# The dense first layers with one 512-column product for both parts of the values

## What is computed

```python
def swiglu(x, w1, w3, w2):
    return (jax.nn.silu(x @ w1) * (x @ w3)) @ w2

x = x + gate1 * diff_attention(h, ...)
h = rms_norm(x, norm2_g[0]) * (1.0 + scale2) + shift2
x = x + gate2 * swiglu(h, ffn_w1[0], ffn_w3[0], ffn_w2[0])
...
x = x + gate1 * gla_mixer(h, ...)
x = x + gate2 * moe_swiglu(h, ...)
```

## Time and profile before

| | |
|---|---|
| median of 3 runs | 1329.33 us (1327.12 to 1330.67) |
| the profiled execution, its own time | 1329.2 us |
| its span, first to last instruction | 1327.2 us |
| busy in the span: PE, DVE, ACT | 1277.0, 914.9, 733.9 us |
| mean granted clock of PE | 0.989 of full speed |
| first layers' dense part, about | 176 to 362 us of the span |

### The profile page before, as it was taken

The page is one execution under the profiler, slowest core; times in us unless marked ns, Lnnn a source line. Parts: engine busy times, 40 slices in busy tenths (PEclk is TensorE's granted clock), DMA queues, the critical chain, the costliest instruction groups (busy, mean ns, idle before and its releaser), DMA issues.

```text
span 1327.2 us, 20642 instructions
## 1 busy us (share of the span) xinstructions
PE 1277.0 (96%) x7966; PEld 946.9 (71%) x7966; DVE 914.9 (69%) x1524; ACT 733.9 (55%) x1266; POOL 11.8 (1%) x47
## 2 busy tenths in 40 slices
PE   7999999999999999999999999998998999889996
PEld 5875899999988987667858888745855755257531
DVE  3688899888887568677869998726957643065411
ACT  4655654444465457677839998626935643055400
POOL 1000000000000010000000000000000000000000
PEclk9999999999999999999999999998999999899999
DMA  9994768988768378999999999999999999999996
GB/s 342 345 364 164 276 226 302 316 317 295 279 233 306 127 268 314 419 417 406 421 415 415 407 412 415 420 418 415 410 421 411 419 418 418 421 405 421 416 421 280
DMA packets 130241, 475.01 MB, mean 358 GB/s; under 512 B 9485, under 2 KB 11674, under 8 KB 107610
## 3 DMA queue, kind: packets, MB, share of 16 engines
q1 hardware_dynamic: 128768, 472.38, 90.6%
q10 hardware_dynamic: 1370, 1.25, 0.3%
HBM read 472.55 MB, written 1.05 MB: 357 GB/s over the span
## 4 chain that ended last, share of the span: by engine, by line
PE 76%; DMA 9%; DVE 7%; SPq 3%; ACT 2%; issue 1%; ACTq 0%; POOL 0%; POOLq 0%; DVEq 0%
PE bank L1894 10%; PE bank L1897 10%; PE bank L1895 10%; DMA ring<-in_moe_w 7%; PE bank L2018 6%; PE bank L1398 3%; PE bank L1395 3%; PE bank L1394 3%; SPq L914 3%; DMA beside_out<-in_moe_w 2%; PE bank L1806 2%; PE bank L1719 2%; PE bank L1142 2%; PE bank L1458 2%; PE bank L1453 2%; PE bank L1451 2%
## 5 line engine op out<-in xcount | busy, mean ns | idle before, releaser
L2512 ACT ACTIVATE hi_first<-ring 128x512 fp32r<-128x512 f32 x156 | 95.9, 632 | 57.9 <-DMA ring<-in_moe_w 34.8
L3199 DVE TENSOR_TENSOR lo_first<-ring,hi_first 128x512 fp32r<-128x512 f32 x156 | 102.6, 691 | 34.5 <-ACT hi_first L2512 34.2
L3199 DVE TENSOR_TENSOR lo_third<-ring,hi_third 128x512 fp32r<-128x512 f32 x150 | 98.0, 687 | 33.3 <-ACT hi_third L2512 32.6
L3199 DVE TENSOR_TENSOR lo_second<-ring,hi_second 128x512 fp32r<-128x512 f32 x154 | 100.5, 687 | 21.6 <-ACT hi_second L2512 20.8
L2512 ACT ACTIVATE hi_second<-ring 128x512 fp32r<-128x512 f32 x154 | 95.6, 632 | 30.2 <-PE bank L1897 24.6
L2512 ACT ACTIVATE hi_third<-ring 128x512 fp32r<-128x512 f32 x150 | 92.6, 632 | 28.7 <-DMA ring<-in_moe_w 13.9
L2804 DVE SCALAR_TENSOR_TENSOR ada_acc<-ring,c_act,ada_acc 128x512 f32<-128x512 f32 x140 | 105.1, 750 | 3.9
L2018 PE MATMUL bank<-ring,work 128*32 128x512 f32 x686 | 90.6, 595 | 5.5 <-DMA ring<-in_moe_w 3.3
L2131 ACT ACTIVATE w_hi<-ring 128x1024 fp32r<-128x1024 f32 x66 | 68.8, 1053 | 46.4 <-PE bank L1458 23.6
L3039 DVE TENSOR_TENSOR w_lo<-ring,w_hi 128x1024 fp32r<-128x1024 f32 x66 | 79.4, 1220 | 10.1 <-ACT w_hi L2131 9.9
L1394 PE MATMUL bank<-hg_hi,w_hi 128*128 128x256 f32 x336 | 82.7, 284 | 0.0
(11 more groups left out here) (609 smaller groups left out, 3195.9 us busy)
## 6 DMA issues: line engine op xcount, KB each, us to landing
ring<-in_moe_w SPq DMA_DIRECT2D x207, 1024.0 KB, 19.3
ring<-in_ada_w SPq DMA_DIRECT2D x24, 2048.0 KB, 11.8
ring<-in_moe_w SPq DMA_DIRECT2D x45, 768.0 KB, 15.8
ring<-in_ffn_w SPq DMA_DIRECT2D x15, 2048.0 KB, 9.4
beside_out<-in_moe_w SPq DMA_DIRECT2D x17, 1024.0 KB, 19.8
beside_h<-in_moe_w SPq DMA_DIRECT2D x16, 1024.0 KB, 19.4
beside_x<-in_moe_w SPq DMA_DIRECT2D x15, 1024.0 KB, 21.0
beside_w<-in_moe_w SPq DMA_DIRECT2D x15, 1024.0 KB, 20.8
```

What stands on the lines that cost most here:

```text
L2512: A(hi_piece(Q), raw_piece(SPLITS[r], q, j), ACT.Copy).then_inc(hi_done, 1)
L3199: v.tensor_tensor(lo_piece(Q), raw_piece(SPLITS[r], q, j), hi_piece(Q).bitcast(F32), ALU.subtract).then_inc(lo_done, 1)
```

## The change

The high weights are multiplied once per `k` with high and low values side by side (512 columns), so that a bank's first half gets the sum of the two high-value products and its second half the low-value product alone. Each piece then takes a whole bank: `w1` bank 5, `w3` bank 4, for every group but group 0, which stays as it was. ACT copies the second half of a bank to the tile of Silu or product, and DVE adds the first half to it, for `w1` and for `w3`; the Silu now reads the sum. PE may start `w1` of a group once the Silu of the group before is made, and `w3` once the product of the group before is made. `hg_hi` and `hg_lo` become the two halves of one tile `hg_both` at the same size.

```diff
--- before.py
+++ after.py
@@ -299,8 +299,8 @@
         lo_second = sb("lo_second", [P, 2, PART], F32R)
         beside_lo = sb("beside_lo", [P, 2 * SUB])
         with ExitStack() as of_norms:
-            hg_hi = of_norms.enter_context(nc.sbuf_tensor("hg_hi", [P, KT, S], F32R))
-            hg_lo = of_norms.enter_context(nc.sbuf_tensor("hg_lo", [P, KT, S], F32R))
+            hg_both = of_norms.enter_context(nc.sbuf_tensor("hg_both", [P, 2, KT, S], F32R))
+            hg_hi, hg_lo = hg_both[:, 0, :, :], hg_both[:, 1, :, :]
         tokens_hi = sb("tokens_hi", [P, 1, SUB], F32R)
         beside_x = sb("beside_x", [P, 2 * SUB])
         tokens_lo = sb("tokens_lo", [P, 1, SUB], F32R)
@@ -725,6 +725,26 @@
             else:
                 eng.wait_ge(g_free, pieces_of_fill(f))
 
+        def hidden_bank(what):
+
+            return psum[5 if what == "w1" else 4]
+
+        def low_copied(what, g):
+
+            return 3 * g - 1 if what == "w1" else 3 * g + 1
+
+        def silu_made(g):
+
+            return 3 * g if g else 1
+
+        def sum_taken(g):
+
+            return 2 * g
+
+        def products_taken(g):
+
+            return 2 * g + 1
+
         def o_place(k):
 
             return (k + 4) % KT
@@ -1383,19 +1403,20 @@
             def hidden(what, f, j):
 
                 q = fpiece[what, f, j]
-                o = 0 if what == "w1" else S
                 g = f * FPC + j
-                if o == 0 and g >= 2:
-                    pe.wait_ge(s_prod, g - 1)
+                if what == "w3":
+                    pe.wait_ge(s_prod, products_taken(g - 1))
+                elif g > 1:
+                    pe.wait_ge(s_silu, silu_made(g - 1))
                 pe.wait_ge(hi_done, q + 1)
                 whi, wlo = split_tile(w_hi, q), split_tile(w_lo, q)
-                out = psum[4 + g % 2][:, o:o + S]
+                bank = hidden_bank(what)
+                both = bank[:, :].rearrange("p (b s) -> p b s", b=2)
                 for k in range(KT):
-                    mm(out, whi[:, k, :], hg_hi[:, k, :], start=(k == 0), stop=False)
-                    mm(out, whi[:, k, :], hg_lo[:, k, :], start=False, stop=False)
+                    mm(both, whi[:, k, :], hg_both[:, :, k, :], start=(k == 0), stop=False, skip_group_check=True)
                 pe.wait_ge(lo_done, q + 1)
                 for k in range(KT):
-                    last = mm(out, wlo[:, k, :], hg_hi[:, k, :], start=False, stop=(k == KT - 1))
+                    last = mm(bank[:, 0:S], wlo[:, k, :], hg_hi[:, k, :], start=False, stop=(k == KT - 1), skip_group_check=True)
                 last.then_inc(w_free, 1)
 
             def first_hidden():
@@ -2378,13 +2399,20 @@
             shift(1)
             for q, (what, f, j) in enumerate(fpieces):
                 split_up_to(q + AHEAD)
+                g = f * FPC + j
+                if what == "w1" and g:
+                    act.wait_ge(w_free, PIECES + q + 1)
+                    A(silu_f[:, g % 4, :], hidden_bank(what)[:, S:2 * S], ACT.Copy).then_inc(s_silu, 1)
                 if what == "w3":
-                    g = f * FPC + j
-                    act.wait_ge(w_free, PIECES + q + 1)
-                    if g >= 4:
-                        act.wait_ge(s_prod, g - 3)
-                    A(silu_f[:, g % 4, :], psum[4 + g % 2][:, 0:S], ACT.Silu).then_inc(s_silu, 1)
-                    act.wait_ge(s_prod, g + 1)
+                    if g == 0:
+                        act.wait_ge(w_free, PIECES + q + 1)
+                        A(silu_f[:, 0, :], psum[4][:, 0:S], ACT.Silu).then_inc(s_silu, 1)
+                    else:
+                        act.wait_ge(s_prod, sum_taken(g))
+                        A(silu_f[:, g % 4, :], silu_f[:, g % 4, :], ACT.Silu).then_inc(s_silu, 1)
+                        act.wait_ge(w_free, PIECES + q + 1)
+                        A(prod_f[:, g % 4, :], hidden_bank(what)[:, S:2 * S], ACT.Copy).then_inc(s_silu, 1)
+                    act.wait_ge(s_prod, products_taken(g))
                     o = j % 2 * S
                     A(hid_hi[:, f % 2, j // 2, o:o + S], prod_f[:, g % 4, :], ACT.Copy).then_inc(s_hidh, 1)
             g_done = [0]
@@ -3083,12 +3111,21 @@
             low_hidden(KT - 1)
             for q, (what, f, j) in enumerate(fpieces):
                 split_up_to(q + AHEAD)
+                g = f * FPC + j
+                if what == "w1" and g:
+                    dve.wait_ge(s_silu, low_copied(what, g))
+                    v.tensor_tensor(silu_f[:, g % 4, :], hidden_bank(what)[:, 0:S], silu_f[:, g % 4, :],
+                                    ALU.add).then_inc(s_prod, 1)
                 if what == "w3":
-                    g = f * FPC + j
                     o = j % 2 * S
-                    dve.wait_ge(s_silu, g + 1)
-                    v.tensor_tensor(prod_f[:, g % 4, :], silu_f[:, g % 4, :], psum[4 + g % 2][:, S:2 * S],
-                                    ALU.mult).then_inc(s_prod, 1)
+                    if g == 0:
+                        dve.wait_ge(s_silu, 1)
+                        v.tensor_tensor(prod_f[:, 0, :], silu_f[:, 0, :], psum[4][:, S:2 * S], ALU.mult).then_inc(s_prod, 1)
+                    else:
+                        dve.wait_ge(s_silu, low_copied(what, g))
+                        link(v.tensor_tensor(prod_f[:, g % 4, :], hidden_bank(what)[:, 0:S], prod_f[:, g % 4, :], ALU.add))
+                        v.tensor_tensor(prod_f[:, g % 4, :], silu_f[:, g % 4, :], prod_f[:, g % 4, :],
+                                        ALU.mult).then_inc(s_prod, 1)
                     ada_steps(4 if f in (0, NCH - 2) else 2)
                     dve.wait_ge(s_hidh, g + 1)
                     v.tensor_tensor(hid_lo[:, f % 2, j // 2, o:o + S], prod_f[:, g % 4, :],
```

## The result

The changed kernel takes 1334.48 us (median of 6 runs, 1332.84 to 1336.03), the kernel before 1329.01 us beside it: ratio 1.0046, with a 95% interval from 1.0037 to 1.0056, or 5.5 us more. The forecast was 1334.5.

What follows compares the result with a forecast made beforehand. PE was taken to bound the dense layers, with DVE barely keeping pace in chunk 0. Stalls of 7.0 + 2.2, 0.5 at the end, minus 4.5 saved gave +5.2 on 1329.3: 1334.5 us, range 1328.5 to 1338.5.

Steps and rivals of the forecast that it cites:

- PE's saving: Dense first layers: 336 pairs of products, each 13.3 ns cheaper as one wide product, 4.5 us in all.
- the prediction's own sign: Check named beforehand: 512-column products start 0.227 us apart; otherwise a price in the forecast is wrong.
- The rival of 240 ns: A 512-column product in two runs costs what two products did; +8.2 us, 1337.5 us, chance 0.12.
- no gain: What the 240 ns price implies: the wide product saves PE nothing; 1337.5 us, chance 0.12.
- that of 215.6 ns: Rival price of the wide product: 8.2 us saved, stalls slightly larger; +2.8 us, 1332.1 us, chance 0.08.
- The stalls: PE waits for DVE's and ACT's results: 7.0 us in the first stretch, 2.2 us in chunk 4.
- DVE's lateness at the end: At the residual closing the dense layers, DVE arrives between nothing and 0.8 us late; taken as 0.5 us.
- The sum: At the end of the dense layers: 7.0 + 2.2 + 0.5 - 4.5 = +5.2 us.
- The loads: Slots left later by DVE shift loads as much as PE; weights keep their four-piece lead, cost nothing.
- The passing on to the end: After the dense layers, the later stages including the expert stage shift by the same amount, +5.2 us.
- the rival by which the expert stage swallows the shift: Weights, not slots, set when the expert stage's stream starts, so the shift is lost; 1330 us, chance 0.11.
- The faster side: Rival: waits do not bind if DVE's period stays under 5.55 us in chunks 0 and 4; 1324.8 us, chance 0.07.

Runs made afterwards that it cites:

- Run 1: The changed kernel without copies and sums, groups taking four banks in turn, low-value products left out of the result; stage -3.59 us, ratio 0.9969 to the kernel before.
- Run 2: The changed kernel with two 256-column products in place of each wide one; stage +8.27 us, ratio 1.0064 to the kernel before.
- run 4: The changed kernel with chunk 4's ada steps shared 2, 2, 6, 6 over its groups instead of 4 each; stage +5.74 us, ratio 1.0048 to the kernel before.
- run 5: run 4 with the load of chunk 4's `w2` weights issued ahead of the last ada load; stage +4.04 us, ratio 1.0036 to the kernel before.
- Run 8: run 3 with three ada steps a group in chunks 0 and 1, and the reduction moved earlier; stage -2.80 us, ratio 0.9978 to the kernel before.
- run 3: The changed kernel with groups taking two pairs of banks in turn, reused two groups later; stage -1.19 us, ratio 0.9998 to the kernel before.

## Why the prediction was right

**PE's saving was too large by 0.9 us.** It was 336 times 13.3 ns, from the expert stage's 226.7 ns. Run 1 gives 10.7 ns a pair. In the changed kernel eight wide products take 1.84 us up to the first low-weight one (206.11 to 207.96), about 230 ns each, so by the prediction's own sign (starts 0.227 us apart) the price was wrong. The expert rows are a long row of equal products; here every eight are followed by eight of 256 columns. Whether that change of width costs the 3 ns was not tried. The rival of 240 ns, and with it "no gain", is ruled out by runs 1 and 2, that of 215.6 ns by the rows above. The some 216 ns at 512 columns in "TensorE: Matmul & The Clock Gate", section "Back-to-back issue gap", in the Trainium skill are given there for an isolated product; in this stream, where eight wide products follow each other with new weights for each, the trace shows about 230.

**The stalls were right in place, number and size.** Predicted 1.5, 2.2, 1.2, 0.9 and 1.2 us; measured 1.40, 2.23, 1.06, 0.80 and 1.05. In chunk 4 predicted about 1.0 and 1.2; measured 0.99 and 1.07. All have the releaser that was named: the first DVE's product, the others ACT's Silu. The reasons for them are DVE's periods, predicted as 6.47 and 6.76, measured as 6.49 and 6.76. The later ones are 0.1 to 0.15 us smaller than said because PE's pieces were a little longer: where DVE sets the pace, what a pair of pieces takes more (2.90 + 2.79 us against 5.55) the stall takes less. The stalls come to 8.6 us, and to 9.3 with the 0.11 us by which the piece after a stall is longer, six times beside the one in the 2.23; the prediction had 9.2 and no such term.

**DVE's lateness at the end** was put at 0.5 us; it is 0.1. The residual starts 1.02 us after the first of the last products (364.56 to 365.58), against 0.92 before (360.74 to 361.66). DVE has made up its arrears by then.

**The sum** is then -3.6 + 9.3 + 0.1 = +5.8, against 5.76 read; the prediction's was -4.5 + 9.2 + 0.5 = +5.2. Two terms were off by 0.9 and 0.4 in opposite directions, so the total is better than its parts, and that is luck. So is the last digit of 1334.5 against 1334.48: the six times of the changed kernel spread over 3.2 us, and the forecast stood on 1329.3 where the kernel before took 1329.01 beside it, which is 5.2 us forecast against 5.5 measured.

**The loads** were costed at nothing, and in the change that is right: PE never waits for weights there, though ACT's longest wait for them is 3.23 us. But the reason, that slots left later shift the loads no more than PE, is not a general one: run 4 broke it by moving four ada steps back by two groups, and run 5 took the late load away.

**The passing on to the end** was right. The dense layers end 3.92 us later in the two profiles (361.66 and 365.58; the one before begins them 1.84 us later). The first product of the expert stage is as much later, 3.93 us, and behind that stage the last products of the program still start 3.61 us later (the first two rows are of the kernel before, the others of the changed one). So the rival by which the expert stage swallows the shift is out, also by the median, +5.5 us, where it had the kernel at 1330:

```profile
509.08 0.47 PE L1894 MATMUL bank<-hi_first,tokens_hi 128*128 128x512 f32 x1
...
1319.14 2.62 PE L2044 MATMUL bank<-work 64*128 64x512 f32 x8 [0.90 <-DVE work L3433]
```

```profile
513.01 0.47 PE L1915 MATMUL bank<-hi_first,tokens_hi 128*128 128x512 f32 x1
...
1322.75 3.95 PE L2065 MATMUL bank<-work 64*128 64x512 f32 x8 [0.90 <-DVE work L3470]
```

**The faster side**, waits that do not bind, had its point of decision named right: DVE's period against PE's. Run 8 is a version in which the waits hardly bind (one stall of 0.48 us is left), by a lead of two groups and an even spread of the steps; it gains 2.8 us in the stage and not 4.5, for the saving is 3.59 and not 4.5.

## What to carry to other kernels

A cheaper product that takes more of the accumulator memory shortens the time between the use of a bank and its next use. Before counting PE's saving, compare the period of the engine that empties the banks, added work included, with PE's new period, stage by stage; if it is longer in some groups, ask by how many groups the wait leads. "Perfetto Trace Analysis", section "Matmuls", in the Trainium skill says that independent groups should rotate through different banks; here two groups' lead instead of one was worth 7.0 us of stage (run 3 against the change), with the same work on every engine.

Work that fills an engine's gaps and also holds a load slot has two prices: moved later, it may free the engine and delay a load that stands behind it in a fixed order (runs 4 and 5).

## What the runs showed of the chip that was not expected

After the stalls of 1.25 and 1.95 us around 180 us the granted clock stayed at 1.00 in the profile of the changed kernel. In that of run 5, with the same two stalls (idle 1.23 and 1.95 us), it fell to 0.50, the 1.2 GHz level, from shortly before 184 to past 186 us (stretches, PE's clock third from the right):

```profile
184.00:185.00 1.00, 1.00 (x3) 0.74 (x3) 0.96 (x3) 0.70 (x2) 0.00 (x0) 0.50 1.00 358
185.00:186.00 1.00, 1.00 (x4) 0.77 (x3) 0.96 (x2) 0.67 (x1) 0.00 (x0) 0.50 1.03 401
...
187.30:190.00 2.70, 2.70 (x18) 2.37 (x17) 2.70 (x4) 1.75 (x3) 0.00 (x0) 1.00 1.03 382
```

The piece after the stall took 4.46 us instead of 2.90. Most of that came off the next stall, since PE was to wait for DVE anyway; the two pieces together were 0.5 us longer (182.84 to 190.08, against 183.21 to 189.96). Run 4's profile shows the same fall behind the same stall (4.46 us from 185.17), and from its first stall to its last one in the first stretch, 180.16 to 205.75, it takes 0.57 us more than the change (178.19 to 203.21). Run 2's profile, with stalls of 1.15 and 1.88 us there, shows 1.00 throughout. Why the clock falls in two of the four profiles stays open.

The last eight products of the program, after a wait, took 2.62 us at a clock of 1.00 in the profile before, but 3.95 us in that of the changed kernel, at 0.50 in their first part. That is 1.3 us of the difference between the two spans, 1327.2 and 1332.5, far from the place of the change; run 8's profile has 2.61 again. The first row is of the kernel before, the second of the changed one:

```profile
1319.00:1321.20 2.20, 2.06 (x8) 1.28 (x8) 1.45 (x3) 0.00 (x0) 0.00 (x0) 1.00 0.03 7
```

```profile
1322.70:1325.00 2.30, 2.25 (x5) 1.70 (x7) 0.80 (x2) 0.00 (x0) 0.00 (x0) 0.50 0.03 7
```

So in this kernel two profiles differed by 0.5 us at one place and 1.3 us at another for the clock alone; the length of the stage, cleared of that, was the measure that closed the sums.
